# A two-layer decoder trunk on one core: the mixers' transposes, value products, rotated scratch and output projection in another order

## What is computed

```python
DEPTH, SEQ, D_MODEL, HEADS, HEAD_DIM = 2, 512, 1024, 16, 64
# layer 0
x = x + 0.5 * gate * swiglu(mod(rms_norm(x)))                       # ffn0
x = x + gate * (moba_attention(rope(h@wq), rope(h@wk), h@wv) @ w_o)  # mixer A
x = x + 0.5 * gate * swiglu(...)                                    # ffn1
kv = mod(rms_norm(x)) @ kv_w        # 3 branches x (k, v), shared
# layer 1
x = x + 0.5 * gate * swiglu(...)                                    # ffn2
x = x + gate * (sum_b w_b * band_attention(rope(h@wq_b), k_b, v_b) @ w_o)  # mixer B
x = x + 0.5 * gate * swiglu(...)                                    # ffn3
out = rms_norm(x)
```

## Time and profile before

| | |
|---|---|
| median of 3 runs | 2506.6 us (2500.38 to 2510.87) |
| the profiled execution | 2512.62 us, of which its span is 2510.8 us |
| PE busy | 2393.7 us, 95% of the span |
| DVE, ACT, POOL busy | 1325.9, 875.2, 250.1 us |
| mean granted TensorE clock | 0.975 |
| mixer A's attention, first score to end of output projection | 456.9 to 708.3 us |
| mixer B's attention, likewise | 1770.2 to 2124.0 us |

### The profile page before, as it was taken

The page is one execution under the profiler, slowest core; times in us unless marked ns, Lnnn a source line. Parts: engine busy times, 40 slices in busy tenths (PEclk is TensorE's granted clock), DMA queues, the critical chain, the costliest instruction groups (busy, mean ns, idle before and its releaser), DMA issues. The chain is left out here.

```text
span 2510.8 us, 31515 instructions
## 1 busy us (share of the span) xinstructions
PE 2393.7 (95%) x11245; PEld 1972.4 (79%) x11245; DVE 1325.9 (53%) x2087; ACT 875.2 (35%) x1397; POOL 250.1 (10%) x322
## 2 busy tenths in 40 slices
PE   9999999898899999999999999999888778999998
PEld 6888888777668888888888888888777666888886
DVE  7555546555565554465544555446665545433333
ACT  3222234445443332233333333223444433433321
POOL 0000000334100000011211000000233311000000
PEclk9999999999899999999999999999999879999999
DMA  6666543766446664336557666437899882233332
GB/s 247 192 190 192 157 126 90 225 181 177 122 132 193 186 188 128 116 105 218 183 193 243 192 183 187 136 117 186 237 231 221 208 195 67 82 99 100 93 100 84
DMA packets 143089, 408.13 MB, mean 163 GB/s; under 512 B 18193, under 2 KB 27025, under 8 KB 142993
## 3 DMA queue, kind: packets, MB, share of 16 engines
q1 hardware_dynamic: 129936, 356.57, 48.9%
q0 software_dynamic: 13056, 50.33, 5.5%
HBM read 352.84 MB, written 52.43 MB: 161 GB/s over the span
## 5 line engine op out<-in xcount | busy, mean ns | idle before, releaser
L372 DVE TENSOR_TENSOR w_lo<-w_raw,w_hi 128x1024 fp32r<-128x1024 f32 (+2 forms) x386 | 471.5, 1222 | 599.5 <-ACT w_hi L368 598.9
L377 PE MATMUL ps<-h_hi,w_hi 128*128 128x512 f32 x1872 | 749.5, 400 | 18.9 <-DVE w_lo L372 6.2
L379 PE MATMUL ps<-h_hi,w_lo 128*128 128x512 f32 x1872 | 737.4, 394 | 0.0
L378 PE MATMUL ps<-h_lo,w_hi 128*128 128x512 f32 x1872 | 736.6, 394 | 0.0
L368 ACT CAST w_hi<-w_raw 128x1024 fp32r<-128x1024 f32 (+2 forms) x388 | 395.7, 1020 | 743.5 <-PE ps L379 729.1
L377 PEld LDWEIGHTS ps<-h_hi,w_hi 128*128 128x128 f32 x1872 | 356.9, 191 | 95.1 <-DVE w_lo L372 11.1
L379 PEld LDWEIGHTS ps<-h_hi,w_lo 128*128 128x128 f32 x1872 | 355.9, 190 | 76.8
L378 PEld LDWEIGHTS ps<-h_lo,w_hi 128*128 128x128 f32 x1872 | 357.3, 191 | 69.6 <-issue 0.2
L377 PE MATMUL ps<-act_hi,w_hi 128*128 128x512 f32 x704 | 275.3, 391 | 0.0
L379 PE MATMUL ps<-act_hi,w_lo 128*128 128x512 f32 x704 | 274.0, 389 | 0.0
L378 PE MATMUL ps<-act_lo,w_hi 128*128 128x512 f32 x704 | 273.9, 389 | 0.0
(11 more groups left out here) (191 smaller groups left out, 2841.9 us busy)
## 6 DMA issues: line engine op xcount, KB each, us to landing
w_raw<-gate_up SPq DMA_DIRECT2D x176, 512.0 KB, 3.9
ada_raw<-ada SPq DMA_DIRECT2D x144, 512.0 KB, 4.6
w_raw<-down SPq DMA_DIRECT2D x80, 512.0 KB, 3.6
w_raw<-kv_w SPq DMA_DIRECT2D x48, 512.0 KB, 3.7
w_raw<-mixa_w SPq DMA_DIRECT2D x34, 512.0 KB, 3.9
w_raw<-mixb_w SPq DMA_DIRECT2D x34, 512.0 KB, 4.8
kb<-rot_st POOLq DMA_DIRECT2D x12, 1024.0 KB, 5.3
k_hi<-kb SPq DMA_DIRECT2D x64, 192.0 KB, 5.6
```

Of the source, the lines that this page charges most:

```text
L372: eng.tensor_tensor(w_lo[:, slot, 0:n], w_raw[:, slot, 0:n], w_hi[:, slot, 0:n].bitcast(F32), ALU.subtract).then_inc(w_lo_done[slot], 2)
L377: nc.tensor.matmul(out_ap, l_hi, r_hi, start=start, stop=False, skip_group_check=skip)
L378: nc.tensor.matmul(out_ap, l_hi, r_lo, start=False, stop=False, skip_group_check=skip)
L379: return nc.tensor.matmul(out_ap, l_lo, r_hi, start=False, stop=stop, skip_group_check=skip)
```

## The change

- The transposed row alternates between banks 6 and 7 (`turned`), and a transposition waits for `pt_lo` of the row two before, no longer of the one before. B's odd scores move from bank 7 to bank 3, the exchange from 3 to 5, which it shares with the value products (`o_ps`), so that it also waits for `att_done` and the value products for `exchanged`.
- A's value products (`weigh_a`) come one step later, with a second pair of tiles for transposed rows (`pt_a`, in free halves of `q_st` and `k_hi`). B's (`weigh_b`) are cut in two: 16 matmuls at the old place in relation to the transpositions, 8 one step later.
- B's LAG goes from 5 to 6 and its slots of probabilities from 6 to 8. POOL scales a row in each step and no longer four in one. `find_gap` moves from the end of DVE's step 4n to the start of step 4n + 1, `joint_factor` behind that step's maximum. `exchange` moves behind the step's transpositions.
- B has four substeps before a group's step 0 (PRE 8) where there were two, and one each in steps 2 and 3 where there were two.
- Scratch in DRAM holds a partition's three branches side by side, so that B's loads of queries and keys are runs of 6 KB, its values' of 4 KB; A's stores are runs of 8 KB. The number of DMAs is the same.
- The output projection begins its tiles 0 and 1 with four rows k; their rows 4 and 5 (parts `0x`, `1x`, with the weights in unused columns of units 6 and 7) come at the end of the steps. Three parts (6 m) stand before the last group after its step 15, where four (8 m) stood, and the output parts begin at step 1 in A and step 2 in B, where they began at steps 4 and 7. The last weight splits and adds move with them. 16 m stand behind the last value products, where 13 did.

The diff, cut to its core:

```diff
-STEPS, EARLY, PRE = 16, 4, 6
-SUBSTEPS = {step: (2 * step + 6, 2 * step + 7) for step in range(4)} | {step: (step + 10,) for step in range(4, 14)}
+STEPS, EARLY = 16, 4
+PRE = {"A": 6, "B": 8}
+SUBSTEPS = {"A": {step: (2 * step + 6, 2 * step + 7) for step in range(4)} | {step: (step + 10,) for step in range(4, 14)},
+            "B": {0: (8, 9), 1: (10, 11)} | {step: (step + 10,) for step in range(2, 14)}}
...
-OUT_PARTS = [(tile, (2 * j, 2 * j + 1)) for tile in range(2, KT) for j in range(OUT_K // 2)]
-OUT_AHEAD = ((0, (0, 1)), (0, (2, 3)), (1, (0, 1, 2, 3)), (0, (4,)), (1, (4,)))
-OUT_LAST = [(0, (5,)), (1, (5,))]
-LAG = {"A": 2, "B": 5}
-SLOTS = {"A": 4, "B": 6}
+OUT_FIRST = 4
...
+OUT_AHEAD = ((0, (0, 1)), (0, (2, 3)), (1, (0, 1)), (1, (2, 3)))
...
+LAG = {"A": 2, "B": 6}
+SLOTS = {"A": 4, "B": 8}
...
 OUT_SUBSTEPS = {
-    "A": {4: OUT_LAST} | {step: OUT_PARTS[2 * step - 10:2 * step - 8] for step in range(5, 10)}
-    | {step: OUT_PARTS[step:step + 1] for step in range(10, 18)},
-    "B": {7: OUT_LAST} | {step: OUT_PARTS[step - 8:step - 7] for step in range(8, 16)}
-    | {step: OUT_PARTS[2 * step - 24:2 * step - 22] for step in range(16, 21)}}
-OUT_HIGH = {"A": {4: 2, 5: 3, 6: 4, 7: 5, 9: 6, 11: 7, 14: 8, 17: 9},
-            "B": {7: 2, 8: 3, 10: 4, 13: 5, 16: 6, 17: 7, 19: 8, 20: 9}}
-OUT_LOW = {"A": {4: 2, 5: 3, 6: 4, 7: 5, 9: 6, 11: 7, 14: 8}, "B": {7: 2, 8: 3, 10: 4, 13: 5, 16: 6, 17: 7, 19: 8}}
-OUT_ADD = {"A": {5: 0, 6: 1, 7: 2, 8: 3, 10: 4, 12: 5, 15: 6}, "B": {8: 0, 9: 1, 11: 2, 14: 3, 17: 4, 18: 5, 20: 6}}
-OUT_IN = {"A": {3: 5, 11: 6}, "B": {6: 5, 14: 6}}
+    "A": out_table({1: "2a", 2: "2b", 3: "3a", 4: "3b", 5: "2c", 6: "3c", 7: "4a", 8: "4b", 9: "4c", 10: "5a", 11: "5b",
+                    12: "5c", 13: "6a", 14: "6b", 16: "6c 0x", 17: "7a 7b", 18: "7c 1x"}),
+    "B": out_table({2: "2a", 3: "2b", 5: "3a", 7: "3b", 10: "2c", 11: "3c", 12: "4a", 13: "4b", 14: "4c", 15: "5a",
+                    16: "5b 5c", 17: "6a", 18: "6b", 19: "6c", 20: "0x 7a", 21: "7b 7c", 22: "1x"})}
+OUT_HIGH = {"A": {0: 2, 1: 3, 5: 4, 6: 5, 9: 6, 12: 7, 16: 8, 18: 9},
+            "B": {0: 2, 1: 3, 10: 4, 11: 5, 14: 6, 16: 7, 20: 8, 22: 9}}
+OUT_LOW = {layer: {step: n for step, n in high.items() if n < 9} for layer, high in OUT_HIGH.items()}
+OUT_ADD = {"A": {0: 0, 1: 1, 6: 2, 7: 3, 10: 4, 13: 5, 17: 6, 19: 7}, "B": {1: 0, 2: 1, 11: 2, 12: 3, 15: 4, 17: 5, 21: 6, 23: 7}}
+OUT_IN = {"A": {4: 5, 12: 6}, "B": {0: 4, 8: 5, 16: 6}}
 POOL_ROWS = (0, 1, 2, 3, 4, 6)
-POOL_LAST = {"A": 12, "B": 15}
-POOL_IN_AHEAD = {"mixA": {11: (0,), 12: (1,), 13: (2,), 14: (3,), 15: (4,)}, "mixB": {12: (0, 1), 13: (2, 3), 15: (4,)}}
+POOL_IN = {"A": {13: 6}, "B": {0: 4, 17: 6}}
...
         def scores(layer, st):
-            return ps[:, 4 if layer == "A" or st % 2 == 0 else 7, :]
-
-        def o_bank(layer, h):
-            return ps[:, 5 if layer == "B" or h % 2 == 0 else 7, :]
+            return ps[:, 4 if layer == "A" or st % 2 == 0 else 3, :]
+
+        def turned(st):
+            return ps[:, 6 + st % 2, :].rearrange("p (n q) -> p n q", n=4)
+
+        o_ps = ps[:, 5, :]
+        def flat(tile):
+            return tile[:].rearrange("p l b s -> p (l b s)")
+
...
+        pt_a = ((pt_hi[:], pt_lo[:]), (second_pt(q_st), second_pt(k_hi)))
...
-        dram_q = {"A": scratch("qa", (G, 1, 2, 2, P, S)), "B": scratch("qb", (G, NB, 2, 2, P, S))}
-        dram_k = {"A": scratch("ka", (G, 1, 2, 2, P, S)), "B": scratch("kb", (G, NB, 2, 2, P, S))}
-        dram_v = {"A": scratch("va", (G, 1, 4, P, TT * 2 * HD)), "B": scratch("vb", (G, NB, 4, P, TT * 2 * HD))}
+        dram_q = {"A": scratch("qa", (G, P, 4, 1, S)), "B": scratch("qb", (G, P, 4, NB, S))}
+        dram_k = {"A": scratch("ka", (G, P, 4, 1, S)), "B": scratch("kb", (G, P, 4, NB, S))}
+        dram_v = {"A": scratch("va", (G, 4, P, 1, TT * 2 * HD)), "B": scratch("vb", (G, 4, P, NB, TT * 2 * HD))}
...
+            extra = tile < 2 and ks[0] >= OUT_FIRST
+            bank, unit, at = tile % 3, tile, 0
+            if extra:
+                bank, unit, at = TAIL_BANK[tile], OUT_K + tile, OUT_K - OUT_FIRST
...
             def exchange(h):
                 pe.wait_ge(spread_ready, 2 * h + 2)
+                if h >= 2:
+                    pe.wait_ge(att_done["B"], h - 1)
...
             def transpose_p(st):
                 pe.wait_ge(scaled_done[layer], st + 1)
-                if st >= 1:
-                    pe.wait_ge(pt_lo_done[layer], st)
+                if st >= 2:
+                    pe.wait_ge(pt_lo_done[layer], st - 1)
...
+            def weigh_b(h, part):
+                if part == 0:
+                    pe.wait_ge(pt_lo_done["B"], 4 * h + 3)
+                    pe.wait_ge(v_landed[h % 2], 8 * HEADS + 80 * (h // 2 + 1))
+                    if h >= 1:
+                        pe.wait_ge(att_done["B"], h)
+                    if h + 1 < HEADS:
+                        pe.wait_ge(exchanged, 2 * h + 3)
+                else:
+                    pe.wait_ge(pt_lo_done["B"], 4 * h + 4)
...
+                back = st - lag
+                if is_a and back >= 5 and back % 4 == 1:
+                    weigh_a(back // 4 - 1)
+                if not is_a and back >= 4 and back % 4 < 2:
+                    weigh_b(back // 4 - 1, back % 4)
+                for part in second:
+                    part()
+                if 0 <= back < ROWS:
+                    transpose_p(back)
                 if not is_a and st % 4 == 0 and 4 <= st <= ROWS:
                     exchange(st // 4 - 1)
-                if (st - lag) % 4 == 0 and st - lag >= 4:
-                    weigh_v((st - lag) // 4 - 1)
-                for part in second:
-                    part()
-                if 0 <= st - lag < ROWS:
-                    transpose_p(st - lag)
 
             def group(g, a, following):
 
@@ -865,8 +918,8 @@
...
-        def load_rows(sp, tile, dram, a, j, copy, part, landed, n_b=None):
-            n_b = dram.shape[1] if n_b is None else n_b
-            for half in range(2):
-                row = 64 * copy + 32 * half
-                sp.dma_start(tile[row:row + 32, j % 2, 0:n_b, :].bitcast(F32),
-                             dram[a, 0:n_b, part, half, 32 * j:32 * j + 32, :]
-                             .rearrange("b i t -> i b t")).then_inc(landed, 16)
+        def load_rows(sp, tile, dram, a, j, copy, part, half, landed, n_b=None):
+            n_b = dram.shape[3] if n_b is None else n_b
+            row = 64 * copy + 32 * half
+            to = tile[row:row + 32, 0, j % 2:j % 2 + 1, :] if dram.shape[3] == 1 else tile[row:row + 32, j % 2, 0:n_b, :]
+            sp.dma_start(to.rearrange("p b t -> p (b t)").bitcast(F32),
+                         dram[a, 32 * j:32 * j + 32, 2 * part + half, 0:n_b, :]
+                         .rearrange("p b t -> p (b t)")).then_inc(landed, 16)
 
...
             def begin(st):
+                joins = not is_a and st % 4 == 1 and 5 <= st <= ROWS + 1
+                if joins:
+                    find_gap(st // 4 - 1)
                 if st < ROWS:
                     negated_max(st)
+                if joins:
+                    joint_factor(st // 4 - 1)
                 if is_a and 1 <= st <= ROWS:
                     invert(st - 1)
                 if not is_a and st % 4 == 0 and 4 <= st <= ROWS:
                     spread(st // 4 - 1)
 
-            def join(st):
-                if not is_a and st % 4 == 0 and 4 <= st <= ROWS:
-                    find_gap(st // 4 - 1)
-
             def collect(st):
-                if (st - lag) % 4 == 0 and st - lag >= 4:
+                if (st - lag) % 4 == 1 and st - lag >= 5:
                     fold_add((st - lag) // 4 - 1)
                 if 0 <= st - lag < ROWS:
                     split_pt(st - lag)
-                if not is_a and st % 4 == 0 and 4 <= st <= ROWS:
-                    joint_factor(st // 4 - 1)
 
             def read_out(g, pair, half):
                 dve.wait_ge(unit_used, g * 6 + u0 + 2 * pair + 2)
...
-                if not is_a and st % 4 == 1 and 5 <= st <= ROWS + 1:
-                    for i in range(4):
-                        scale(st - 5 + i)
+                if not is_a and 5 <= st < ROWS + 5:
+                    scale(st - 5)
```

229 lines of the change are left out of this document (125 added, 104 removed).

## The result

The changed kernel took **2479.81 us** (median of 4, 2474.59 to 2481.78); the kernel before, beside it, 2506.18 (2500.38 to 2510.87). The ratio is 0.989, with a 95% interval of 0.9875 to 0.9904. The forecast was 2442 us: the direction is right, the range holds the time, but the gain is 26 us where 65 were forecast. The rival in which "the ring holds everything" (a ring: ACT and DVE passing each row to and fro through their own written orders) had said 2483.

The account below looks back on a forecast made before the run. It bounded the attention groups by the ACT and DVE ring (66.6 us per full B group) and PE's work (63). Gains of 43.2 + 25.7 = 68.9 less 3.5 gave 65 us: 2442 us, range 2405 to 2490.

Parts of the forecast that it names:

- the ring holds everything: Rival, chance 0.19: ACT and DVE set the steps, the second bank only moves PE's wait to the scores; 24 us, 2483.
- I put each group halfway between its bound and its time before: Attention groups of both mixers: each gains half its room, or half its idle time and clock; 43.2 + 25.7 us.
- Value products one step later: Both mixers: a step's work now covers PE's waits of 10.8 and 11.4 us for pt_lo; under 4 to stay.
- Substeps: B's group starts: 2.7 us more cover cuts 4.8 us waits to about 2 in two groups; last stays 4 to 5.
- SP's queue: B's value loads wait two steps later on SP's queue: 2 us taken off the forecast sum.
- the slower rival: Rival, chance 0.06: SP's in-order queue delays B's query rows and later heads' keys and values, 75 us together; 2517 us.
- its deciding point: B's group starts: the slower rival decides if direct rows are issued over about 3 us after their split; before, 0.02.
- Transpositions, two banks: Both mixers: transpositions wait for the split a whole step before; all 21.0 us of their waits can go.
- What the ring leaves: B's full group: ACT and DVE need 66.6 us, PE 63; none below some 67; middle groups gain 7.8 and 10.9.
- Scratch runs: DRAM scratch loads: longer runs should relieve DMA engines, but the sum takes nothing; bounds 0 to 10 us.
- Output projection: Last groups: earlier output parts give PE work in empty steps; gains 19.5 us in B, 12.9 in A; end wait goes.

Follow-up runs that it names:

- best3: Changed kernel, A's value products one step earlier, B's substep 12 in step 3, value loads one place later, last group's second-head values behind fourth-head keys: 2456.17 us.
- b_pre6: Changed kernel with mixer B's old substep table: six substeps ahead of a group's first step, two in each of steps 0 to 3: 2470.88 us.
- b_substeps: Changed kernel with mixer B's projection substep 12 moved from step 2 to step 3: 2464.67 us.
- b_poolorder: Changed kernel with B's row 3 of the output projection's input cast a step earlier, ahead of the third pair's rope, on POOL and DVE: 2476.23 us.
- a_w_old: Changed kernel with only mixer A's value products put back one step earlier, its two transposed banks kept: 2470.76 us.
- a_undone: Changed kernel with mixer A's transpositions waiting for the row just before again and its value products one step earlier: 2468.75 us.
- best2: Changed kernel, A's value products one step earlier, B's substep 12 in step 3, value loads one place later, row 3's cast earlier on POOL: 2455.71 us.
- b_sporder: Changed kernel with mixer B's value loads one place later on SP's queue, so no key load stands behind their wait: 2469.47 us.

## Why the prediction was wrong, and where it was right

The forecast is a sum of 68.9 us by groups less 3.5. Against the profiled groups:

- **The step that failed** is "I put each group halfway between its bound and its time before", for the middle groups of B and all of A. B's middle groups were to gain 7.8 and 10.9 us and gained 0.6 and 5.5; A's four groups were to gain 4.2, 2.6, 6.0 and 12.9 and gained -1.7, -1.1, 1.3 and 4.1. The rule priced a difference of two bounds and never asked what each moved instruction now stands behind. Three were put in worse places, and each can be named, with what undoing it gave by the medians and by its mixer's length: A's value products out of step 14 (9 and 7 us), substep 12 ahead of the reading out (15 and 13.6), the value loads' wait on SP's queue (10 and 7). Undone together they gave 24 us of the 38 by which the kernel missed its forecast. The 14 left lie mostly in A: best3's trace has 14.7 us of the 25.7 forecast for A and 41.7 of B's 43.2. Why A's half of its idle time and clock does not come stays open.
- **Value products one step later: the wrong sign.** "Before, A's stood straight behind the last transposition's rounding and split", and that 10.8 us wait went. But it was a wait in a step that has nothing else to do. The prediction named the maximum that frees the score bank as late next, under its two banks, and did not price it: 25.5 us more of L801.
- **Substeps: right for two, silent on the third.** The cover ahead of the direct rows brought 3 to 6 us where 5.4 were counted (b_pre6 against b_substeps), and their wait fell from 4.7 and 4.8 us to 2.96 and 2.98 where about 2 was said. The third was to stay at 4 to 5 and shows 1.8, but only because PE had just stood 4.8 us for POOL's `h_lo`; in b_poolorder, without that wait, it is 6.4. "The m are not new; steps 2 and 3 lose them" passed over which m stays in step 2: the one that needs a bank read out.
- **SP's queue: the mechanism of the slower rival, at a smaller price.** It took 2 us in the sum. The direct rows were not held up, so its deciding point was not reached; but the third head's keys and queries were, and the order cost 7 to 10 us.
- **Transpositions, two banks: the wait went, the gain did not.** All 43.2 us for `pt_lo` are gone, as promised, and the bank is worth 3.3 us. In A the ring rival's sentence holds, that the bank only moves PE's wait to the scores; in B the waits for the maximum did not grow. The Trainium skill (TensorE: Matmul & The Clock Gate, "HAM oscillation") says of a kernel that double-buffering in PSUM gave no further gain; that was another kernel, with waits for DMA. This case agrees in A (a_w_old against a_undone) and nearly so in B (3.3 us).
- **What the ring leaves: too heavy in the rival, about right in the forecast.** 35.3 us more of DVE cost 12. With the placements repaired B gained 41.7 us in best3's trace (353.8 to 312.1) and 49.4 in best2's, the fastest of its executions (304.4), where 43.2 were forecast; best3's middle groups came to 73.3 and 76.8, inside the 72 to 80 that were to show the forecast right. In A the rule stays too high by about half: 12.7 us (251.4 to 238.7, best2) or 14.7 (best3) of 25.7.
- **Scratch runs: right.** Nothing was taken for them, and they are worth nothing measurable. The Trainium skill (DMA: Bandwidth & Descriptors, "Why small descriptors are slow") names an overhead from which little was to be expected at 2 KB; the run with 2 KB runs agrees (0.7 us), and the landing times that seemed to speak against it follow mostly the order of issues (8.2 us before, 7.1 with the old runs in the new order, 6.8 changed).
- **Output projection: right in size in B, not in A.** B's last group gained 16.4 us where 19.5 were forecast, with the clock from 0.82 to 0.91. A's gained 4.1 where 12.9 were forecast (8.6 in best3), though its clock went from 0.87 to 0.93. The beginning of B's last group shows it best: before and after, from the group's start on, some eight and a half steps of the one and just over twelve of the other:

```profile
2010.70:2050.00 39.30, 29.87 (x144) 27.40 (x145) 17.43 (x69) 15.89 (x49) 7.89 (x17) 0.64 0.79 187
```

```profile
1996.70:2045.00 48.30, 39.09 (x243) 35.39 (x244) 27.36 (x97) 24.51 (x72) 15.06 (x28) 0.86 0.87 228
```

  In 39.3 us before, PE ran 144 matmuls at a clock of 0.64; now 243 in 48.3 us at 0.86. The prediction's two marks, a clock above 0.9 in both last groups (0.93 and 0.91) and no wait at A's end for the add of a part, were met. How much of it is the table of output parts, and how much the lag of six rows and the cut of the value products, was not tried: these hold each other in order, and none could be undone alone without rewriting the others.

The ring rival came within 4 us of the time by a cancellation. It took the bank for worthless, which it nearly is, and counted 24 us for the covers and the last groups, which about came (16.4 and 4.1 in the last groups, 3 to 6 for the cover). That the other edits would lose some 24 us at three places, and that about as much would come from the rest of the change, it did not say; which part brought that, the cut value products, the lag or the spread multiplies, was not tried.

## What to carry to other kernels

Price a moved instruction by what it now stands behind and by what stood in its old place, not by the wait that it leaves: a wait in a step without other work may cost nothing, and work that fills such a step (here 8 matmuls, 7 to 9 us) should stay there. When a table moves work earlier, look up which of its items is the first to need something freed; a single entry one step early cost more than the second bank, the longer runs and the cover brought together. And if "the ring sets the rows" is a theory, charge it: add a known time to the ring in every row and see what share comes out.

## What the runs showed of the hardware

- A short wait of PE can cost more than its length, and not in every execution. In steps 2 and 3 of one group the changed kernel and b_substeps have the same matmuls: 2.8 us of idle time went and 4.4 us with it, and the granted clock in the step of the wait was 0.82 with it and 1.00 without. In step 0 of the same group PE stands behind a wait for the direct rows and then does the same 25 matmuls in every trace: behind 3.10 us of wait they took 4.1 us at a clock of 1.00 (a_undone), behind 2.96 us 5.7 at 0.70 (the changed kernel), behind 2.95 us 6.9 at 0.57 (a_w_old).
- A transfer's landing time was the queue's state and not its own shape: 64 KB value loads landed in 2.0 us under either scratch layout and in 6.1 us in b_sporder, where they are issued behind keys and queries; the third head's 192 KB query loads landed in 7.5 us behind the values and beside a 1 MB store, and in 5.8 us ahead of both.
